# A two-block transformer kernel: one modulation chunk behind the attention, a projected tile in two parts, the experts' first rounds in another order

## What is computed

```python
def first_block(x, c, ...):
    c_act = jax.nn.silu(c)
    mod = (c_act @ w_ada[l] + b_ada[l])[:, None, :]
    sh1, sc1, g1, sh2, sc2, g2 = jnp.split(mod, 6, axis=-1)
    h = rmsnorm(x, norm1_g[l]) * (1.0 + sc1) + sh1
    ... = jnp.split(h @ w_in[l], offsets, axis=-1)
    o_hg = hgrn2_mixer(...)          # recurrent branch, 4 heads of 128
    o_nsa = nsa_mixer(...)           # compressed, selected and window attention, 8 heads of 64
    x = x + g1 * (jnp.concatenate([o_hg, o_nsa], axis=-1) @ w_out[l])
    h = rmsnorm(x, norm2_g[l]) * (1.0 + sc2) + sh2
    x = x + g2 * moe_ffn(h, ...)     # 64 experts, 8 per token, and a shared one
    return rmsnorm(x, final_g)

def second_block(x, c, w_mod, b_mod, ...):
    c_act = jax.nn.silu(c)
    for l in range(2):
        mod = (c_act @ w_mod[l] + b_mod[l]).reshape(c.shape[0], 9, 1024)
        ...                          # feed-forward, mixer, feed-forward, each normed and modulated
```

## Time and profile before

| | |
|---|---|
| median of 3 runs | 3124.35 us (3122.42 to 3128.5) |
| the profiled execution, its own time | 3126.24 us |
| its span, first to last instruction | 3124.3 us |
| mean granted clock of TensorE | 0.981 of full |
| TensorE busy | 2974.5 us, 95% |
| VectorE busy | 1686.7 us, 54% |
| ScalarE busy | 1122.5 us, 36% |
| GpSimd busy | 329.0 us, 11% |

### The profile page before, as it was taken

The page is one execution under the profiler, slowest core; times in us unless marked ns, Lnnn a source line. Parts: engine busy times, 40 slices in busy tenths (PEclk is TensorE's granted clock), DMA queues, the critical chain, the costliest instruction groups (busy, mean ns, idle before and its releaser), DMA issues. The chain is left out here.

```text
span 3124.3 us, 39167 instructions
## 1 busy us (share of the span) xinstructions
PE 2974.5 (95%) x13974; PEld 2316.1 (74%) x13974; DVE 1686.7 (54%) x1833; ACT 1122.5 (36%) x1354; POOL 329.0 (11%) x425
## 2 busy tenths in 40 slices
PE   6999797999999998999999999999999999999998
PEld 4876565767767666888877778887888877778886
DVE  6745936777777756555346565523555246543322
ACT  3124633556555542222235422212222125433211
POOL 0100001344442220000000000000000000000000
PEclk9999998999999998999999999999999999999999
DMA  7552316999999976554222155422544221122221
GB/s 282 168 172 106 108 75 219 358 355 362 369 357 348 356 264 274 202 188 162 95 98 69 67 189 188 175 95 73 209 181 169 95 98 68 68 94 94 94 94 68
DMA packets 115275, 554.57 MB, mean 177 GB/s; under 512 B 20593, under 2 KB 22130, under 8 KB 72946
## 3 DMA queue, kind: packets, MB, share of 16 engines
q1 hardware_dynamic: 88690, 490.39, 42.6%
q0 software_dynamic: 26496, 62.96, 5.8%
HBM read 548.06 MB, written 37.75 MB: 187 GB/s over the span
## 5 line engine op out<-in xcount | busy, mean ns | idle before, releaser
L184 DVE TENSOR_TENSOR stream_low<-stream_raw,stream_high 128x2048 fp32r<-128x2048 f32 x156 | 356.8, 2287 | 411.6 <-ACT stream_high L179 411.2
L179 ACT ACTIVATE stream_high<-stream_raw 128x2048 fp32r<-128x2048 f32 x151 | 289.2, 1916 | 801.3 <-PE ffn_ps_psum L569 756.7
L567 PE MATMUL ffn_ps_psum<-h_high_f,stream_high 128*128 128x512 f32 x1344 | 525.0, 391 | 0.0
L569 PE MATMUL ffn_ps_psum<-h_high_f,stream_low 128*128 128x512 f32 x1344 | 523.1, 389 | 0.0
L568 PE MATMUL ffn_ps_psum<-h_low_f,stream_high 128*128 128x512 f32 x1344 | 522.9, 389 | 0.0
L322 DVE TENSOR_TENSOR expert_low<-expert_raw,expert_high 128x2048 fp32r<-128x2048 f32 x128 | 293.5, 2293 | 183.7 <-ACT expert_high L318 183.6
L318 ACT ACTIVATE expert_high<-expert_raw 128x2048 fp32r<-128x2048 f32 x128 | 244.2, 1908 | 144.8 <-PE experts_g_psum L569 144.8
L569 PEld LDWEIGHTS ffn_ps_psum<-h_high_f,stream_low 128*128 128x128 f32 x1344 | 252.3, 188 | 53.0
L568 PEld LDWEIGHTS ffn_ps_psum<-h_low_f,stream_high 128*128 128x128 f32 x1344 | 252.4, 188 | 52.3 <-issue 0.2
L567 PEld LDWEIGHTS ffn_ps_psum<-h_high_f,stream_high 128*128 128x128 f32 x1344 | 252.4, 188 | 51.9 <-issue 0.2
L801 DVE TENSOR_TENSOR ffn_sg<-ffn_sg,ffn_ps_psum 128x512 f32<-128x512 f32 x88 | 60.5, 688 | 416.6 <-PE ffn_ps_psum L569 409.8
(11 more groups left out here) (458 smaller groups left out, 4660.6 us busy)
## 6 DMA issues: line engine op xcount, KB each, us to landing
expert_raw<-in_exp_gu SPq DMA_DIRECT2D x128, 1024.0 KB, 8.9
stream_raw<-in_ffn_gu SPq DMA_DIRECT2D x88, 1024.0 KB, 4.9
expert_raw<-in_exp_dn SPq DMA_DIRECT2D x64, 1024.0 KB, 7.6
con<-in_w_mod SPq DMA_DIRECT2D x120, 512.0 KB, 5.6
stream_raw<-in_ffn_dn SPq DMA_DIRECT2D x44, 1024.0 KB, 5.0
mix_mod_rows<-in_w_ada POOLq DMA_DIRECT2D x32, 512.0 KB, 4.7
stream_raw<-in_w_in SPq DMA_DIRECT2D x16, 1024.0 KB, 4.9
pieces_raw<-in_w_in SPq DMA_DIRECT2D x13, 1024.0 KB, 6.5
```

Source lines behind the costliest of these rows:

```text
L179: self.nc.scalar.activation(self.high[:, q], self.raw[:, q], ACT.Copy).then_inc(self.high_done, 1)
L184: self.nc.vector.tensor_tensor(self.low[:, q], self.raw[:, q], self.high[:, q].bitcast(F32), ALU.subtract)\
L567: mm(out, w[0], x[0], start=start, stop=False)
L569: return mm(out, w[1], x[0], start=False, stop=stop)
```

## The change

1. **Projected tile.** `project(25)` is made in two parts: three of its eight steps, then `score(0)`, then the other five.
2. **Modulation.** Chunk 1 of `mod_c` leaves the loop. VectorE multiplies all its eight pieces in a row behind `out_to_low(0)`, ahead of the splits of pieces 19 and 20. TensorE's reduction stands between the first five output tiles and the last three, and writes to the bank that tile 7 uses.
3. **Late blocks.** The 18 operations on tokens beyond a block's 128 leave the routing and stand among the first rounds of the experts on VectorE; GpSimd, SyncE's queue and the others wait for them only where they read the number of blocks.
4. **First rounds.** The first rounds of the experts are written out by hand on TensorE, ScalarE and VectorE, and the loop starts at 1.
5. **Idle products.** Two instead of one at the mixer's end, three instead of one at the routing's start, two instead of none at the experts' start.

```diff
@@ Modulation
+    def reduce(self, pe, g, ps=None):
+        ps = self.ps if ps is None else ps
...
@@ first_mixer
-            FIRST_BESIDE = (6, 15)
+            FIRST_BESIDE, LAST_REDUCED = 6, bank(6)
...
-                    project(25)
...
                         if i == 0:
+
+                            pe.wait_ge(evacuated, place(IN_TILES - 2) + 1)
+                            pe.wait_ge(roped, 6)
+                        elif i == 1:
                             pe.wait_ge(evacuated, place(IN_TILES - 1) + 1)
                             pe.wait_ge(cmp_masked, 1)
-                            pe.wait_ge(roped, 6)
...
+                    project(25, range(3))
                     for i in range(ITEMS + 2):
                         if i < ITEMS:
                             score(i)
                         if i == 0:
+                            project(25, range(3, KD))
                             mod(mod_b, 0, "mod4")
-                        elif i == FIRST_BESIDE[1]:
+                        elif i == FIRST_BESIDE + KD + 1:
                             mod(mod_c, 0, "mod5")
-                        elif i == ITEMS:
-                            mod(mod_c, 1, "mod6")
...
                     pe.wait_ge(copied, ITEMS)
+                    pe.wait_ge(out_low, TT)
+                    mod_c.reduce(pe, 1, LAST_REDUCED)
                     for n in range(5, KD):
                         if n == 7:
-                            pe.wait_ge(out_low, TT)
+                            pe.wait_ge(last_finished, 1)
...
                     out_to_low(0)
+                    mod_c.multiply(dve, 1, range(KD))
+                    mod_c.finish(dve, 1, LAST_REDUCED).then_inc(last_finished, 1)
                     split(19)
                     split(20)
@@ experts, pe
+                    for _ in range(2):
+                        idle_products(self, pe, psY[:, 0, :])
+                    for n in range(2):
+                        turn_x(0, n)
+                    table(1, 0)
+                    gate_up(0, 0)
+                    table(1, 1)
+                    for s in range(2):
+                        gate_up((s + 1) // 2, (s + 1) % 2)
+                        turn_h(0, s)
+                        turn_x(1, s)
+                        table(2 + s, 0)
+                        down(0, s)
+                        table(2 + s, 1)
@@ experts, act
+                    copy_x(0, 0)
+                    copy_x(0, 1)
+                    split(0, 1, 0)
+                    silu(0, 0)
+                    split(0, 1, 1)
@@ experts, dve
+                    split(0, 0, 1)
+                    copy_x(0, 0)
+                    for n in range(2):
+                        compare(1, n)
+                    copy_x(0, 1)
+                    read(1, 0)
+                    find_late_blocks()
+                    split(0, 1, 0)
+                    hidden(0, 0)
+                    read(1, 1)
+                    compare(2, 0)
+                    split(0, 1, 1)
+                    place_late_pairs()
+
+                    for s in range(2):
+                        split(1, s, 0)
+                        hidden((s + 1) // 2, (s + 1) % 2)
+                        copy_x(1, s)
+                        read(2 + s, 0)
+                        compare(2 + s, 1)
+                        split(1, s, 1)
+                        copy_y(0, s)
+                        read(2 + s, 1)
+                        if s == 0:
+                            compare(3, 0)
```

More of the change, by code:

```diff
@@ L2182, in route @@
             wr, sg = self.sb("wr", [P, KD, E]), self.sb("shared_sg", [P, S])
-            order, part = self.sb("order", [P, TT, E]), self.sb("part", [P, TT, E])
-            nb, incl, first = (self.sb(x, [P, E]) for x in "nb incl first".split())
-            junk, eb = self.sb("junk", [P, E]), self.sb("eb", [P, 1])
-            half, rest, spare = self.sb("half", [P, 1]), self.sb("rest", [P, NBLK // 2]), self.sb("spare", [P, 1])
             logits = self.sb("logits", [E, S])
@@ L2406, in _ @@
-                    chain(v.tensor_scalar(first[:], first[:], float(E - 1), None, ALU.add))
-                    chain(v.tensor_tensor(part[:], order[:], first[:].unsqueeze(1).broadcast_to([P, TT, E]), ALU.add))
-                    chain(v.scalar_tensor_tensor(out=part[:], in0=order[:], scalar=1.0, in1=part[:], op0=ALU.is_ge, op1=ALU.mult))
-                    chain(v.tensor_tensor(tables.block[:], part[:], tables.picked[:], ALU.mult))
                     dve.wait_ge(up, 2)
@@ L2442, in used, with pipelined @@
             def used(eng):
+                eng.wait_ge(late_found, 1)
                 return eng.value_load(used_pairs[0:1, 0:1], min_val=R_ALWAYS, max_val=R)
[L2445 to L2454 removed]
+            def pipelined(eng, steps, late_steps=None, start=0):
+                with eng.Fori(start, FIRST) as r:
                     for s in range(2):
```

111 lines of the change are left out of this document (56 added, 55 removed).

## The result

| | before | after |
|---|---|---|
| median | 3124.35 us (3121.42 to 3134.47, 20 runs) | 3131.18 us (3127.06 to 3140.85, 20 runs) |
| the profiled execution, its own time | 3126.24 us | 3130.11 us |
| its span | 3124.3 us | 3128.3 us |
| mean granted clock | 0.981 | 0.982 |

The ratio after to before is 1.0021, 95% interval 1.0014 to 1.0027: the change makes the kernel slower by 4 to 8 us. The interval is clear of no change, but it reaches across the prediction's line of 0.2%, so on which side of it the change lies stays open. The forecast was 3125 (3120 to 3130 for itself, 3118 to 3133.5 with its rivals).

The account below looks back on a forecast made before the run. TensorE was taken as the bound, busy 95% of the span. Terms 1.1 - 6.2 + 14.8 + 3.5 - 1.3 - 2.2 - 8.9 = +0.8 gave about 3125 us as median, own range 3120 to 3130, with rivals 3118 to 3133.5.

Parts of the forecast that it names:

- the prediction's line of 0.2%: Whole kernel: a difference of 0.2%, 6.2 us, is about what a measurement can tell from none.
- the four signs: TensorE idle about 13 us before the reduction; multiplication pairs 5.5 apart; last masks 3 to 5 closer; third block after 24 to 27.
- The tile, +1.1: Attention loop's start: first scores stand before tile 25's last five steps, so the first mask comes 1.1 us later.
- The loop, -6.2: Attention loop: eight multiplications and the reduction leave, saving 6.2 us; bounds -4.5 and -9.
- The chunk behind the attention, +14.8: Output projection: TensorE waits for three load round trips of 5.5 us, then does the reduction; 14.8 us more.
- Half clock behind it, +3.5: Output projection after the wait: reduction and products at half clock, 3.5 us more; bounds 0 and +4.5.
- Idle products at the routing's start, -1.3: Routing's start: shorter gap keeps full clock for idle products and logits, 1.3 us less.
- Late blocks out of the routing, -2.2: Routing's end: without VectorE's late-block work, the stage ends with the shared expert's product, 2.2 us sooner.
- First rounds of the experts, -8.9: Experts' start to third block's products: 26.4 us instead of 35.3 in the new order; bounds 25.1 and 31.
- the rival that I gave 0.22: Routing's and experts' starts: idle products run at half clock ahead of the work, +7.1 together, 3132 us; chance 0.22.
- the gain outweighs: Rival: loop gives all 9, less half clock behind it, experts lose no clock; -6.9 in all, 3117.5 us; chance 0.2.
- Slower loads: Rival for the chunk's wait behind the attention: loads at the earlier modulation's pace, 2.5 us longer, 3128 us; chance 0.08.

Follow-up runs that it names:

- experiment 1: Modulation chunk back in the attention loop, reduction in round 24, against the changed kernel: 3116.04 us, ratio 0.9968.
- experiment 9: Modulation chunk in the attention loop instead of six multiplications ahead of `out_to_low(0)`, against the kernel of experiment 8: 3112.65 us, ratio 0.9958.
- experiment 2: Four of the chunk's eight multiplications ahead of `out_to_low(0)`, against the changed kernel: 3121.60 us, ratio 0.9986.
- experiment 7: Six of the chunk's multiplications ahead of `out_to_low(0)`, two behind, against the changed kernel: 3116.05 us, ratio 0.9979.
- experiment 12: The chunk's reduction two output tiles later, against the kernel of experiment 8: 3110.76 us, ratio 0.995.
- experiment 6: One idle product each at the mixer's end and routing's start, experts' two kept, against the changed kernel: 3131.57 us, ratio 1.0031.
- experiment 4: Second block's gather at the head of the experts instead of the routing's end, against the changed kernel: 3135.36 us, ratio 1.003.
- experiment 8: Six multiplications ahead, no idle products in experts, tile whole, both indices before the gathers, against the changed kernel: 3110.20 us, ratio 0.9959.
- experiment 10: Late-block work back on VectorE in the routing, experts' new first rounds kept, against the changed kernel: 3129.44 us, ratio 1.0012.
- experiment 3: Without the two idle products at the experts' start, against the changed kernel: 3127.15 us, ratio 1.0007.
- experiment 5: Last projected tile in one part again, first scores behind it, against the changed kernel: 3134.57 us, ratio 1.0039.

## Why the prediction was right, and where not

The median, 3131.18, lies in the range, and above the forecast's own range (3120 to 3130). That it stayed in is in part luck. The upper end of the range had been drawn for a rival, of which one half came true; the rest of the miss comes from a step that was wrong (the routing's end) and from a loop that gave less. The mechanism behind the largest term, TensorE's wait for the chunk, was right. Of the four signs that the prediction named, three came: the idle stretch (14.04 us), round trips near 5.5 us (5.0 to 5.3) and the last masks 4.2 to 4.7 us closer. The fourth did not: the third block's products came 29.50 us after the experts' start, not 24 to 27. One sum in it is off: by the bounds it states, all high ones together give +13.3, which is 3137.7 and not near 3135. Step by step:

- **The tile, +1.1: right.** +1.30 at the first mask in every kernel with the split tile (17.49 to 17.51 against 16.18 to 16.21).
- **The loop, -6.2: right in kind, too large.** It gave 4.46, at the lower bound of 4.5; experiments 1 and 9 give 3.9 and 4.7. Over all profiles this stretch takes 105.4 to 108.0 us without the chunk in the loop (eleven) and 110.75 to 111.4 with it (three), so a single difference of this kind is good to about 1.3 us. By the masks, the first multiplication was free, as I had said; the next four gave 3.7 instead of 4.8, and the last three 1.2 instead of 0.7. The other error is the reduction that left round 24, for which I took 0.7: TensorE waits for ScalarE's copy there (1.92 us), and nothing was gained. The rest, 0.5, was lost at the loop's two ends.
- **The chunk behind the attention, +14.8: right.** The wait of 14.04 and the reduction's 1.95 make 16.0. VectorE needed 19.6 us for its eight pieces instead of 18.4. The round trips were shorter than 5.5 (4.97, 5.29, 5.34), but the odd pieces landed up to 1.5 us behind the time at which VectorE could take them, and the last one is on the path. Landings took 3.7 to 4.5 us. By the Trainium skill (DMA: Bandwidth & Descriptors, Anatomy of one DMA) they would have been an estimated 3.2; the trace does not agree, and the sum with the page's figure would have been further off. Experiments 1, 2, 7 and 12 show that this wait is the loss, and that it follows the number of round trips that stand behind `out_to_low(0)`: three, one begun late, and one that is covered give 14.0, 3.3 and 0 to 3.0 us.
- **Half clock behind it, +3.5: right.** 1.5 on the reduction (3.41 us to the next product, where I had 1.95) and 1.9 from there to the mixer's end, less 0.3 on the products ahead of the wait: 3.0.
- **Idle products at the routing's start, -1.3: right.** -1.61, and experiment 6 gives 1.65 back. The gap shrank to 1.58 us and not to 1.3, so it was not below the 1.5 us that I had leaned on; the clock held all the same.
- **Late blocks out of the routing, -2.2: wrong.** "The stage's end is then the shared expert's product right behind TensorE": it is not. The stage ends when GpSimd's second gather has landed, though no instruction of the routing waits for it; only TensorE's turning in the next stage does. That gather is issued 2.06 us after the first, for its index is cast behind it, at 495.58 in the changed kernel; 4.7 us later it has landed, and 0.9 us after that the next stage runs. In experiments 1 and 4, where the last gather took 4.5 and 4.2 us to land, the next stage follows 1.0 us after the landing, and in experiment 8 1.2 us; from the end of the gather's issue the same times are 4.1 to 4.9 us, so the landing fits better than a fixed time from the issue. Before the change the second gather was issued at 484.79; its landing there is an estimate from the 4.2 to 4.7 us of the others, at 489.0 to 489.5. That coincides nearly with VectorE's end at 489.28, and so the profile put the blame on VectorE. Experiment 10 shows that 2.5 us more of VectorE change nothing, experiment 4 that the gather does. I had looked for what ended last among the engines, and not at the transfers in flight.
- **First rounds of the experts, -8.9: mechanism right, one term wrong.** The new order does what I had said, and most of the 8.9 came (5.78). What failed is that the stage was counted "all at full clock". Since the routing's end did not move up, TensorE had been idle for 4.1 us, and the clock was at 0.50 at the start. The miss of 3.1 has two halves. For the idle products I had 1.7; they took 3.75 us and stood ahead of everything, and experiment 3 gives 3.2 back: 1.5. Without them I would have had 24.7 us (26.4 less 1.7), and experiment 3 measured 26.30, with both turnings at 1.94 where I had counted full clock: 1.6. That a shorter gap would have kept the clock is seen in experiment 4: behind 1.59 us the same two idle products took 1.96 us and the first turning 1.04. This is the experts' half of the rival that I gave 0.22; its other half, the routing, did not happen. Its deciding point, the clock when they begin, was the right one.

The sum was +0.8 and the segments show +8.2: 3.1 from the experts, 1.9 from the routing's end, 1.7 from the loop, 0.7 from the chunk and its clock, 0.2 from the tile, less 0.3 from the routing's start. The medians, 6.8 apart, agree with 8.2 within the scatter of the parts that were not changed. Of the rivals, the one in which the gain outweighs is out. Slower loads came half true: 1.2 us of the 2.5.

## What to carry to other kernels

Work that is moved into an idle stretch of one engine brings its loads along. With two slots, eight pieces are three round trips of 5.0 to 5.3 us, and these have to fit into the stretch, not the multiplications alone; start them as far ahead as the engine has gaps, and put the step that consumes the sum behind the last work that does not need its bank. Before pricing what an engine's last work in a stage costs, look for the last transfer that was issued and when it lands: here a gather held the stage's end, and taking 6.5 us of work away moved it by 0.3. An idle product is work in front of work. Here the added ones gained 1.65 us at the routing's start, where the gap ahead shrank from 2.1 to 1.6 us and the clock read 1.00 when they began, and cost 3.2 us at the experts' start, behind a gap of 4.1 us, where it read 0.50.

## What the runs showed that I had not expected

A gather of 128 rows by GpSimd landed in 4.2 to 4.7 us when little else moved, and in 11.1 us when SyncE's queue issued two loads of a megabyte 1.5 us after it (experiment 4). In the experts' first rounds other gathers took 8.1 us (before the change, at 498.42) and 9.7 and 10.6 us (experiment 8). The Trainium skill (DMA: Bandwidth & Descriptors, SWDGE vs HWDGE vs iDMA) says that each DMA engine takes turns between the queues of the two kinds. From 503 to 517 us in experiment 4 the packets of SyncE's queue held 7.3 KB on average (2.10 MB in 288) and GpSimd's 2.5 KB (0.36 MB in 144), so turns packet by packet would favour the loads. That this is what delayed the gather is an argument; no run here shows the turns themselves.

The clock at the experts' start did not follow the gap alone: after 4.2 us without a product the first turning ran at 1.07 us in the profile of experiment 9 and at 1.94 in those of experiments 3 and 8, which have the same instructions there. With the idle products in front it was the same: behind 4.1 to 4.3 us the first turning ran at 1.04 in experiments 2, 6 and 7, and behind 3.9 to 4.1 us at 1.91 or 1.92 in the changed kernel and experiments 1, 5 and 10. What decides between them stays open.
